# Gathered expert rows summed by four 64x64 products on TensorE's quarters in place of two products of the whole array

## The chip, the core and the metric

The program runs on one core of one Trainium2 chip. The metric is the time of one execution on the device, in microseconds (us). The engines are TensorE (PE in the profile, PEld for its weight loads), VectorE (DVE), ScalarE (ACT), GpSimd (POOL) and SyncE (SP), and 16 DMA engines move data between HBM and on-chip memory.

## What is computed

One layer of a decoder trunk on 1024 tokens of 1024 features: a mixer (latent attention, a recurrent branch, differential attention), cross-attention to a memory, and a retrieval FFN. The change touches only the last step of the FFN. Cut to this:

```python
def peer_ffn(h, w_q, keys, u, v):
    # ... experts (b, s, 8 heads, 16) and gates g from product keys; n_blk = 8 blocks of 128 tokens
    def block(args):
        xt, et, gt = args
        act = jax.nn.gelu(jnp.einsum('td,thkd->thk', xt, u[et]), approximate=False)
        return jnp.einsum('thk,thkd->td', gt * act, v[et])
```

For every token 128 rows of u (1024 floats each) are gathered and multiplied with the token's h, and 128 rows of v are gathered and added up with the weights gt * act. All is float32.

## The kernel before, in words

The tokens go in 8 blocks of 128, one token to a partition. Each block has a *front* (norms, projections, attention, recurrence, cross-attention, the choice of experts) and a *retrieval*. The retrieval of block b-1 runs through the front of block b: the class `Pace` places its 128 positions between the pieces of the front, on PE, ACT and DVE each, by tables of stops written out by hand (`TENSOR_STOPS`, `VECTOR_STOPS`, `SCALAR_STOPS`). The last retrieval runs alone after the last front.

At position p of the retrieval, for a block of 128 tokens:

- POOL gathers one u row per token (`gather_u`, L810) and one v row per token (`gather_v`, L824), each a 128x1024 tile, into rings of 9 slots. `gather_v` waits until the row that held the slot has been summed (`v_used`, counted by PE, or `v_added`, counted by DVE).
- DVE multiplies the u row with h and reduces it to a dot product (L2052).
- ACT turns 8 dot products into activations (L1516), DVE multiplies them with the gates to `coef` (L2084), and ACT builds for each row a diagonal matrix `diag` = identity scaled by that row's coefficient per token (L1528; four buffers).
- PE adds the v row to the running sum `ps_sum` (two PSUM banks of 128x512) as `diag` times the v row, at L1267 in `add_row`. Every eighth row goes instead to DVE (L2074), and in the last 24 positions of the last block every second one, so that 887 rows are summed on PE.
- After a block's last row DVE adds `ps_sum` to `x_cur` (`sum_out`, L2092), PE waits for this (`fin_sum`) before it starts the next block's sum, and ACT and DVE do the final norm from `x_cur`.

Lines of the front that the text names, all on PE: L999 and L1018 are projections, L1066, L1067 and L1071 the projections up from the latents (L1067 has 64 rows of the array), L1114 and L1118 attention scores (L1118 has 32 rows), L1100 turns of the probabilities, L1126 probabilities times values, L1181 the output projections; L1905 is a DVE add of a 128x512 PSUM bank. A float32 product appears in the trace as two weight loads and two matmul records, so a row of L1267 is four of each. `w_ring` holds the weights that SP streams from HBM.

Of the kernel before, what the change touches and what calls it, by code (L numbers as in the profile page):

```python
# [16 lines left out]
ALU = mybir.AluOpType  # L17
# [28 lines left out]
HALF = 512  # L46
# [49 lines left out]
def on_vector(b, j):  # L96

    return j % SHARE == SHARE - 1 or (b == NB - 1 and j >= TAIL and j % 2)


def adds_before(b, j):

    return sum(on_vector((b * EXPERTS + j - 1 - i) // EXPERTS, (j - 1 - i) % EXPERTS) for i in range(b * EXPERTS + j))


def sums_before(b, j):

    return b * EXPERTS + j - adds_before(b, j)
# [180 lines left out]
def program(nc, x, wstream, columns, w_uq, w_ukv, w_gates, keys_t, ffn_gain, final_gain, mem, positions, pos_cols,  # L289
            rel_bias, diff_lambda, peer_u, peer_v, out):  # L290
    with ExitStack() as ctx:
        def sb(name, shape, dt=F32):
            return ctx.enter_context(nc.sbuf_tensor(name, shape, dt))

        def pb(name, cols):
            return ctx.enter_context(nc.psum_tensor(name, [P, cols], F32))

        def sem(name):
            return ctx.enter_context(nc.semaphore(name))
# [3 lines left out]
        u_rows, v_rows = rows[:, 0:U_RING, :], rows[:, U_RING:U_RING + V_RING, :]  # L303
# [17 lines left out]
        x_cur = sb("x_cur", [P, D])  # L321
# [26 lines left out]
        diag = sb("diag", [P, 4, P])  # L348
# [42 lines left out]
        ps_sum = pb("ps_sum", D)  # L391
# [58 lines left out]
        fin_sum, fin_sq, fin_made, fin_stored = sem("fin_sum"), sem("fin_sq"), sem("fin_made"), sem("fin_stored")  # L450
# [21 lines left out]
        def ge(eng, semaphore, value):  # L472

            if isinstance(value, int) and value <= 0:
                return
            eng.wait_ge(semaphore, value)
# [72 lines left out]
        def row_of(bp, p, lag):  # L549

            j = p - lag
            if j >= 0:
                return (bp, j) if j < EXPERTS else (bp, None)
            return (bp, None) if isinstance(bp, int) and bp == 0 else (bp - 1, j + EXPERTS)

        def row_slot(b, j, ring):

            return (b * EXPERTS + j) % ring

        def row_landings(b, j, ring):  # L560

            return 16 * ((b * EXPERTS + j) // ring + 1)
# [359 lines left out]
        def _(pe):  # L922
# [333 lines left out]
            def add_row(bp, p):  # L1256
                bp, j = row_of(bp, p, SUM_LAG)
                if j is not None and not on_vector(bp, j):
                    n = sums_before(bp, j)
                    pe.wait_ge(diag_made, n + 1)  # L1260
                    slot = row_slot(bp, j, V_RING)
                    pe.wait_ge(v_landed[slot], row_landings(bp, j, V_RING))
                    if j == 0:

                        ge(pe, fin_sum, bp)
                    for c in range(2):
                        ins = pe.matmul(ps_sum[:, c * 512:(c + 1) * 512], diag[:, n % 4, :], v_rows[:, slot, c * 512:(c + 1) * 512],  # L1267
                                        start=(j == 0), stop=(n == sums_before(bp + 1, 0) - 1), skip_group_check=True)
                    ins.then_inc(v_used, 1)

# [16 lines left out]
            def first_mla():  # L1287
                pe.wait_ge(cleared, 6)
                mla(0, 0)

            pace = Pace(add_row, opening, TENSOR_STOPS)
            pace.run(front | {"project_0": lambda b: first_project(), "project_1": lambda b: second_project(),
                              "mla_up": lambda b: first_up(), "mla_0": lambda b: first_mla()}, 0)
# [281 lines left out]
        def _(dve):  # L1575
# [478 lines left out]
            def position(bp, p):  # L2054
                if p < EXPERTS:
                    multiply_row(bp, p)
                if ends_block(bp, p, SUM_AT):
                    sum_out(bp - 1)
                    hand_last_ids(bp)
# [28 lines left out]
            def sum_out(bp):  # L2088

                dve.wait_ge(v_used, sums_before(bp + 1, 0) + SUM_SLOTS)  # L2090
                dve.wait_ge(v_added, adds_before(bp + 1, 0) + ADD_SLOTS)
                dve.tensor_tensor(x_cur[:, :], x_cur[:, :], ps_sum[:, :], ALU.add).then_inc(fin_sum, 1)  # L2092

            def scale_out(bp):

# [39 lines left out]
            pace.start(NB - 1)  # L2135
            pace.to(END)
            sum_out(NB - 1)
            scale_out(NB - 1)

# [81 lines left out]
```

## Time and profile before

| | |
|---|---|
| runs (3) | 3477.66, 3482.75, 3485.28 us, median 3482.75 |
| profiled execution | span 3488.4 us (no other time is shown for it) |
| PE busy | 2948.9 us, 85% |
| DVE, POOL, ACT busy | 2349.6, 2015.7, 812.5 us |
| L1267, the sums on PE | 3548 matmul records, busy 1727.6 us |
| DMA | 1345 MB, mean 386 GB/s over the span |

Busy time is the time in which an engine had an instruction running. The ends of matmuls are modelled, so neighbouring starts are the better measure of a matmul's rate. A window gives, for a stretch of the span, the busy time of each engine with the number of instructions, the granted TensorE clock as a share of 2.4 GHz, and what DMA moved.

### The profile page before, as it was taken

The numbers are of one execution on the slowest core, as the hardware profiler recorded it, in microseconds if no ns is written. First come the engines' busy times: TensorE is split into PE (matmuls) and PEld (weight loads), VectorE is DVE, ScalarE is ACT, GpSimd is POOL, SyncE is SP. The second block draws the span as 40 slices with busy tenths as digits, with TensorE's granted clock in tenths as the row PEclk, the third lists the DMA queues.
The fourth block names the chain that finished last, engine by engine and source line by source line (L and its number), as shares of the span: only waits on it lengthen the run. The fifth ranks groups of instructions, "written<-read, shape, count | busy, mean of one in ns | idle before, by whom it ended". The sixth has DMA issues, their size and how long they took to land.

```text
span 3488.4 us, 34790 instructions
## 1 busy us (share of the span) xinstructions
PE 2948.9 (85%) x10984; PEld 1651.9 (47%) x10984; DVE 2349.6 (67%) x5893; ACT 812.5 (23%) x1915; POOL 2015.7 (58%) x2085
## 2 busy tenths in 40 slices
PE   7876898888988898889997899888998889976675
PEld 6465455544545355534554456444564445522222
DVE  6229846886588765886578765886648865596555
ACT  3111411132211421133211322114221232211111
POOL 1004755666566765666565655665556655477775
PEclk9898999999999999999999999998999999999998
DMA  7788999999999999999999999999999999999998
GB/s 279 277 274 313 408 409 409 408 409 409 409 407 406 394 409 409 408 407 382 409 409 408 392 356 409 409 409 348 359 409 409 409 355 342 385 404 410 409 409 347
DMA packets 386971, 1345.09 MB, mean 386 GB/s; under 512 B 41762, under 2 KB 44834, under 8 KB 386148
## 3 DMA queue, kind: packets, MB, share of 16 engines
q0 software_dynamic: 294912, 1073.87, 78.1%
q1 hardware_dynamic: 90724, 264.79, 20.0%
q10 hardware_dynamic: 1152, 4.19, 0.3%
q8 instruction: 90, 1.47, 0.2%
q14 instruction: 93, 0.76, 0.1%
HBM read 1332.99 MB, written 35.39 MB: 392 GB/s over the span
## 4 chain that ended last, share of the span: by engine, by line
PE 38%; DMA 30%; DVE 15%; POOL 9%; issue 6%; ACT 3%; SPq 1%; DVEq 0%; POOLq 0%; ACTq 0%
PE ps_sum L1267 18%; DMA rows<-in_peer_u,ids_u 13%; DMA rows<-in_peer_v,ids_v 10%; PE ps_p L999 5%; POOL rows L824 5%; POOL rows L810 4%; DVE rows L2052 4%; PE ps_s L1181 4%; DMA rows<-in_peer_v,ids_u 3%; DMA w_ring<-packed 3%; PE ps_s L1118 2%; PE ps_p L1126 2%; DVE feat_b L1935 1%; DVE feat_b L1931 1%; PE ps_s L1114 1%
## 5 line engine op out<-in xcount | busy, mean ns | idle before, releaser
L1267 PE MATMUL ps_sum<-rows,diag 128*128 128x512 f32 x3548 | 1727.6, 629 | 267.1 <-DMA rows<-in_peer_v,ids_v 141.4
L2052 DVE CUSTOM_DVE_ANT_0 rows<-h_cur,rows 128x1024 f32<-128x1024 f32 x1024 | 1226.8, 1220 | 496.3 <-DMA rows<-in_peer_u,ids_u 483.3
L810 POOL DMA_INDIRECT rows<-in_peer_u,ids_u x1024 | 1012.3, 989 | 702.0 <-issue 483.3
L1267 PEld LDWEIGHTS ps_sum<-rows,diag 128*128 128x128 f32 x3548 | 671.0, 200 | 1155.7 <-issue 1005.7
L824 POOL DMA_INDIRECT rows<-in_peer_v,ids_v x512 | 490.3, 958 | 433.8 <-PE ps_sum L1267 277.6
L824 POOL DMA_INDIRECT rows<-in_peer_v,ids_u x512 | 498.2, 973 | 284.7 <-PE ps_sum L1267 144.2
L1528 ACT ACTIVATE diag<-ident,acts 128x128 f32<-128x128 f32 x887 | 324.7, 394 | 1049.4 <-PE ps_sum L1267 750.1
L999 PE MATMUL ps_p<-hT,w_ring 128*128 128x128 f32 x2944 | 358.7, 282 | 28.8 <-DMA w_ring<-packed 15.3
L999 PEld LDWEIGHTS ps_p<-hT,w_ring 128*128 128x128 f32 x2944 | 353.0, 198 | 61.2 <-issue 39.7
L1834 DVE CUSTOM_DVE_ANT_0 e<-ps_s,bias_t 128x256 f32<-128x256 f32 (+6 forms) x96 | 74.2, 773 | 176.3 <-PE ps_s L1118 73.7
L2074 DVE SCALAR_TENSOR_TENSOR x_cur<-rows,acts,x_cur 128x1024 f32<-128x1024 f32 x137 | 175.6, 1282 | 7.4 <-DMA rows<-in_peer_v,ids_v 7.3
L1905 DVE TENSOR_TENSOR x_next<-x_next,ps_s 128x512 f32<-128x512 f32 x32 | 21.9, 685 | 200.0 <-PE ps_s L1181 200.0
L1516 ACT ACTIVATE acts<-dots 128x8 f32<-128x8 f32 x128 | 26.6, 208 | 486.9 <-DVE dots L2052 486.6
L1181 PE MATMUL ps_s<-w_ring,hT 128*128 128x512 f32 x256 | 118.3, 608 | 14.2 <-DMA w_ring<-packed 7.4
L1441 ACT ACTIVATE e<-e,small 128x256 f32<-128x256 f32 (+6 forms) x96 | 75.4, 785 | 219.7 <-DVE small L1836 219.4
L999 PE MATMUL ps_p<-pT,w_ring 128*128 128x128 f32 x1024 | 118.8, 276 | 0.9 <-DMA w_ring<-packed 0.9
L999 PEld LDWEIGHTS ps_p<-pT,w_ring 128*128 128x128 f32 x1024 | 116.9, 192 | 5.4 <-issue 3.3
L1181 PE MATMUL ps_s<-w_ring,feat_b 128*128 128x512 f32 x256 | 114.8, 592 | 1.1 <-DMA w_ring<-in_wstream 1.1
L1935 DVE FIND_INDEX8 feat_b<-feat_b,e 128x8 uint32<-128x128 f32 (+1 forms) x384 | 103.4, 279 | 0.0
L1118 PE MATMUL ps_s<-k_diff,feat_a 32*128 32x512 f32 (+2 forms) x192 | 83.7, 543 | 16.9 <-DVE small L1836 16.8
L1314 ACT ACTIVATE feat_a<-ps_p 128x512 f32<-128x512 f32 (+2 forms) x48 | 26.0, 542 | 304.6 <-PE ps_p L999 304.5
L2052 DVE DVE_READ_ACCUMULATOR2_ANT dots<- 128x1 f32 x1024 | 84.4, 82 | 0.0
(288 smaller groups left out, 2376.2 us busy)
## 6 DMA issues: line engine op xcount, KB each, us to landing
w_ring<-packed SPq DMA_DIRECT2D x343, 512.0 KB
w_ring<-in_wstream SPq DMA_DIRECT2D x65, 512.0 KB
packed<-in_wstream SPq DMA_DIRECT2D x49, 512.0 KB, 8.2
rows<-in_peer_u,ids_u POOLq DMA_INDIRECT x1024, 14.9
rows<-in_peer_v,ids_u POOLq DMA_INDIRECT x512, 12.6
rows<-in_peer_v,ids_v POOLq DMA_INDIRECT x512, 19.3
bias_rows<-rows SPq DMA_DIRECT2D x5, 1024.0 KB, 12.1
bias_t<-in_x SPq DMA_DIRECT2D x8, 512.0 KB, 7.9
```

The costliest lines, as they stand in the source:

```text
L810: pool.indirect_dma_start(u_rows[:, slot, :], None, peer_u, bass.IndirectOffsetOnAxis(ap=ids_u[:, j:j + 1], axis=0)).then_inc(u_landed[slo ...
L824: pool.indirect_dma_start(v_rows[:, slot, :], None, peer_v, bass.IndirectOffsetOnAxis(ap=ids[:, j:j + 1], axis=0)).then_inc(v_landed[slot] ...
L999: ins = pe.matmul(dst, w[:, k, :], lhs[:, kt, :], start=(kt == 0), stop=(kt == KT - 1))
L1118: ins = pe.matmul(ps_s[:, c0:c1], q_diff[r:r + DK, half // 4, :], k_diff[r:r + DK, half // 4, c0:c1], start=True, stop=True)
L1181: pe.matmul(ps_s[:, n * 512:(n + 1) * 512], lhs[:, kt, :], w, start=(kt == 0), stop=(kt == KT - 1)).then_inc(w_used, 1)
L1267: ins = pe.matmul(ps_sum[:, c * 512:(c + 1) * 512], diag[:, n % 4, :], v_rows[:, slot, c * 512:(c + 1) * 512], start=(j == 0), stop=(n == ...
L1441: act.activation(buf[:, 0:keys_n], buf[:, 0:keys_n], ACT.Exp, bias=small[:, 32 + n:33 + n], accum_out=small[:, 48 + n:49 + n]).then_inc(s_ ...
L1528: act.activation(diag[:, n % 4, :], ident[:, :], ACT.Copy, scale=coef[:, j:j + 1]).then_inc(diag_made, 1)
L1834: run(dve.tensor_tensor_reduce(buf[:, 0:keys_n], ps_s[:, 0:keys_n], bias[:, 0:keys_n], 1.0, -3.0e38, ALU.add, ALU.max, small[:, 16 + n:17 ...
L1935: dve.max_index(i[:, first:first + 8], v[:, first:first + 8], s).then_inc(top_step, 1)
L2052: dve.tensor_tensor_reduce(row, h_cur[:, :], row, 1.0, 0.0, ALU.mult, ALU.add, dots[:, p:p + 1]).then_inc(u_used, 1)
L2074: dve.scalar_tensor_tensor(x_cur[:, :], v_rows[:, slot, :], coef[:, j:j + 1], x_cur[:, :], ALU.mult, ALU.add)\
```

## The change

In `add_row` each v row is now four products. Product (c, r) takes the row half r of the partitions (64 tokens) and column half c of the features; its weights are the 64x64 block of `diag` on that half, and its result goes to partitions 64c to 64c+63 of bank r of `ps_sum`. So the partition half of `ps_sum` now tells the column half of the output, and the bank tells the token half. In `sum_out` the one add becomes four that put the quarters back to their places in `x_cur`.

```diff
-                    for c in range(2):
-                        ins = pe.matmul(ps_sum[:, c * 512:(c + 1) * 512], diag[:, n % 4, :], v_rows[:, slot, c * 512:(c + 1) * 512],
+                    for c, r in ((0, 0), (0, 1), (1, 0), (1, 1)):
+                        own = slice(64 * r, 64 * r + 64)
+                        ins = pe.matmul(ps_sum[64 * c:64 * c + 64, r * HALF:(r + 1) * HALF], diag[own, n % 4, own],
+                                        v_rows[own, slot, c * HALF:(c + 1) * HALF],
                                         start=(j == 0), stop=(n == sums_before(bp + 1, 0) - 1), skip_group_check=True)
                     ins.then_inc(v_used, 1)
@@ sum_out
-                dve.tensor_tensor(x_cur[:, :], x_cur[:, :], ps_sum[:, :], ALU.add).then_inc(fin_sum, 1)
+                for c, r in ((0, 0), (1, 1), (0, 1), (1, 0)):
+                    own = x_cur[64 * r:64 * r + 64, c * HALF:(c + 1) * HALF]
+                    ins = dve.tensor_tensor(own, ps_sum[64 * c:64 * c + 64, r * HALF:(r + 1) * HALF], own, ALU.add)
+                ins.then_inc(fin_sum, 1)
```

Nothing is moved: the rows of the retrieval stand between the same pieces of the front. What stands on PE in the attention stage of block 6 (`e` the probabilities, `pT` their turn, `feat_a` queries, `rows` with the v row and `diag` the diagonal; xN counts matmuls of the source) was before:

```order
L1100 MATMUL ps_p<-ident,e 128x128 x7
L1267 MATMUL ps_sum<-rows,diag 128x512 x2
L1126 MATMUL ps_p<-v_mla,pT 128x64 x7
L1118 MATMUL ps_s<-k_diff,feat_a 128x512
L1118 MATMUL ps_s<-k_diff,feat_a 128x384
L1267 MATMUL ps_sum<-rows,diag 128x512 x2
L1118 MATMUL ps_s<-k_diff,feat_a 128x512
```

and is now:

```order
L1100 MATMUL ps_p<-ident,e 128x128 x7
L1268 MATMUL ps_sum<-rows,diag 64x512 x4
L1126 MATMUL ps_p<-v_mla,pT 128x64 x7
L1118 MATMUL ps_s<-k_diff,feat_a 128x512
L1118 MATMUL ps_s<-k_diff,feat_a 128x384
L1268 MATMUL ps_sum<-rows,diag 64x512 x4
L1118 MATMUL ps_s<-k_diff,feat_a 128x512
```

The runs of sums stay where they were, 45 in each of the blocks' bodies but the first (43) and the last (37), and each now has other forms on both sides. A product of the source is two loads and two matmuls in the built program, directly behind one another, so that both passes of one quarter stand ahead of the first pass of the next.

## Rows read from the trace of the kernel before

**Rows 1.** The page: busy time (us), share of the span, instructions.

```profile
PE 2948.9 (85%) x10984; PEld 1651.9 (47%) x10984; DVE 2349.6 (67%) x5893; ACT 812.5 (23%) x1915; POOL 2015.7 (58%) x2085
```

**Rows 2.** Windows of 100 us, from the span's start; the first line names the columns.

```profile
core 0: us, PE busy (x) PEld busy (x) DVE busy (x) ACT busy (x) POOL busy (x), PEclk, DMA share, GB/s
...
1200.00:1300.00 100.00, 95.99 (x364) 53.26 (x363) 60.98 (x137) 26.74 (x62) 62.92 (x65) 1.00 1.01 396
...
1600.00:1700.00 100.00, 94.38 (x371) 53.61 (x372) 63.20 (x140) 27.80 (x63) 60.78 (x62) 1.00 1.01 391
...
2000.00:2100.00 100.00, 94.93 (x331) 50.20 (x331) 60.54 (x138) 31.35 (x67) 56.13 (x59) 0.97 0.94 354
2100.00:2200.00 100.00, 95.65 (x416) 59.33 (x415) 50.53 (x126) 22.57 (x51) 56.50 (x59) 1.00 1.03 409
...
2400.00:2500.00 100.00, 93.77 (x299) 48.36 (x298) 56.50 (x121) 33.49 (x64) 50.66 (x51) 0.91 0.87 312
2500.00:2600.00 100.00, 98.39 (x448) 62.28 (x447) 53.07 (x104) 21.14 (x52) 58.25 (x62) 1.00 1.03 409
...
2800.00:2900.00 100.00, 86.55 (x324) 46.11 (x323) 63.95 (x126) 40.92 (x74) 54.30 (x56) 0.98 0.92 341
2900.00:3000.00 100.00, 98.68 (x374) 57.13 (x374) 51.13 (x111) 20.10 (x48) 54.32 (x58) 0.97 0.95 370
3000.00:3100.00 100.00, 82.53 (x281) 43.53 (x279) 73.32 (x220) 15.11 (x38) 58.94 (x61) 0.97 0.98 383
```

**Rows 3.** Timeline, PE in the last retrieval: start us, us, what, [idle before].

```profile
3210.42 1.95 PE L1267 MATMUL ps_sum<-rows,diag 128*128 128x512 f32 x4 [0.61 <-DMA rows<-in_peer_v,ids_u]
...
3212.98 1.95 PE L1267 MATMUL ps_sum<-rows,diag 128*128 128x512 f32 x4 [0.61 <-DMA rows<-in_peer_v,ids_u]
```

**Rows 4.** Chain that ended last, window 2400 to 2500 us, shares by line.

```profile
by line: PE ps_sum L1267 43.8%; PE ps_s L1118 13.6%; PE ps_p L1126 12.2%; PE ps_p L1100 7.1%; DMA w_ring<-packed 6.0%; PE ps_s L1181 5.4%; ACT pT L1314 4.1%; PE ps_s L1114 3.1%; DVE e L1867 1.2%; ACT e L1441 1.1%; DVE e L1834 1.1%; issue 0.
```

**Rows 5.** Waits, whole span: who for whom, us in total, times, longest.

```profile
POOL rows L824 <- PE ps_sum L1267: 421.8, 244, 12.0
```

**Rows 6.** Timeline, PE in an attention stage; "128*128" is the part of the array.

```profile
2421.54 3.42 PE L1267 MATMUL ps_sum<-rows,diag 128*128 128x512 f32 x4
...
2428.09 1.98 PE L1267 MATMUL ps_sum<-rows,diag 128*128 128x512 f32 x4
2430.00 1.77 PE L1118 MATMUL ps_s<-k_diff,feat_a 32*128 32x512 f32 x4
...
2436.91 1.88 PE L1267 MATMUL ps_sum<-rows,diag 128*128 128x512 f32 x4
2438.63 1.67 PE L1126 MATMUL ps_p<-v_diff,pT 128*128 128x64 f32 x14
2440.23 1.77 PE L1118 MATMUL ps_s<-k_diff,feat_a 32*128 32x512 f32 x4
```

**Rows 7.** Timeline, PE, two lines that alternate between parts of the array.

```profile
2328.66 0.49 PE L1066 MATMUL ps_p<-feat_a,wuq 128*128 128x128 f32 x2
2329.08 0.48 PE L1067 MATMUL ps_p<-feat_a,wuq 64*128 64x128 f32 x2
```

**Rows 8.** Groups: out<-in xcount, busy us, mean ns, idle before with releasers.

```profile
L999 PE MATMUL ps_p<-hT,w_ring 128*128 128x128 f32 x2944 | 358.7, 282 | 28.8 <-DMA w_ring<-packed 15.3 <-DVE hT L1742 13.2
```

**Rows 9.** DVE adds from PSUM, by line: ns min/median/max, first and last start.

```profile
L2092 DVE TENSOR_TENSOR x_cur<-x_cur,ps_sum x8: 1214/1219/1221, 727.1 to 3479.6; 128x1024 f32<-128x1024 f32 x8
...
L1905 DVE TENSOR_TENSOR x_next<-x_next,ps_s x32: 677/686/689, 170.3 to 3005.2; 128x512 f32<-128x512 f32 x32
```

**Rows 10.** Windows of L1267 alone: window, us, PE and PEld busy, PEclk, DMA.

```profile
2000.00:2100.00 100.00, 51.95 (x108) 20.55 (x109) 0.97 0.94 354
2400.00:2500.00 100.00, 49.07 (x95) 18.53 (x93) 0.91 0.87 312
2800.00:2900.00 100.00, 42.75 (x88) 15.81 (x88) 0.98 0.92 341
```

**Rows 11.** A window near the end, columns as in rows 2.

```profile
3440.00:3450.00 10.00, 7.27 (x10) 2.26 (x9) 7.17 (x12) 1.60 (x5) 7.72 (x8) 0.57 1.03 409
```

## The prediction

> **What bounds the kernel now.** I read the windows first, since the one share that the page gives PE, 85% [rows 1], mixes stages. Where sums run, DMA is mostly the limit: at its full share it moves 409 GB/s, as in the windows from 2100 and 2500 us, and a window that shows less lost time [rows 2]. Each position of the retrieval brings one u row and one v row of 128 tokens, and in the last block, where nothing else runs on PE, the sums start 2.56 us apart, each after a wait of about 0.6 us for its row [rows 3]. There PE is busy 1.95 us of 2.56 and a faster sum brings nothing.
>
> The windows in which DMA falls short are all windows in which PE is nearly full [rows 2]: 354 GB/s at 94.93 us busy, 312 at 93.77, 341 at 86.55, 370 at 98.68, 383 at 82.53, and 396 and 391 at 95.99 and 94.38 in two earlier ones. Written as time lost, (409 - GB/s) / 409 x 100 us, these are 13.4, 23.7, 16.6, 9.5, 6.4, 3.2 and 4.4 us, together **77 us**. The dips fall in the attention and cross stages of the later blocks. The chain of waits there names the sums with 43.8% of the window, then the front's own products on PE (L1118, L1126, L1100), then little else [rows 4]. The link to DMA is the ring of v rows: the gather at L824 waited 421.8 us in all for a sum at L1267 to release its slot, ahead of every other wait on this ring [rows 5]. The opening runs below 409 GB/s too, but has no sums, and the change can't reach it. So a PE that costs nothing would bring at most 77 us, and the end of the kernel is reached through DMA.
>
> **What a sum costs.** One gathered row is two instructions in the source, four matmuls in the trace (each f32 product is done as two loads of weights and two passes of the moving rows). Four of them follow one another at 1.72 us when the next work has the same form (2436.91 to 2438.63 [rows 6]), so 0.43 us each. Where the granted clock falls to its lower level, 1.2 GHz, the same four take twice this, 3.42 us from first start to last end (at 2421.54 [rows 6]).
>
> **What is changed, part by part.** Per row PE gets eight loads and eight matmuls in place of four and four, each matmul still with 512 moving columns. A matmul's time follows its columns and not its height: four of the 32x512 form at L1118 are busy 1.77 us, four of the full 128x512 form 1.88 [rows 6]. One product of 64x64 therefore streams for 2 x 0.43 = 0.85 us, and all hangs on **how many of the four run at the same time**. They use four different quarters of the array, the two upper and the two lower row halves write to different banks, and nothing in the program orders them. The trace of before has no place where two products stand on disjoint parts of the array, so the price is bounded from both sides: all four together, 0.85 us a row; one after the other, 4 x 0.85 = 3.41 us.
>
> Full overlap also needs 8 loads and 8 matmuls to be issued in 0.85 us. The densest pairs in these rows are the 14 of L1126, which take 1.60 us from their start to the next line's, 0.114 us a pair (2438.63 to 2440.23 [rows 6]), and eight such pairs are 0.91 us; most of this is the load of 128 columns, where the new ones have 64. I take **0.90 us a row**, a saving of 1.71 - 0.90 = 0.81 us.
>
> The Trainium skill bears on this (TensorE: Matmul & The Clock Gate, Part 3, Packing small matmuls): it reports 16 tiles of 32x32 at 10.6 times the rate of one after the other, which would be the full overlap. No run here shows it, and nothing says that it was f32.
>
> **Switches of form.** The rows stand between the products of the front, which use the full array, in 45 runs a block, mostly of one to three rows (the order listing). Where neighbours differ in form today, it costs: L1066 and L1067 alternate between 128 and 64 rows, and start 0.42 us apart for two 128-column matmuls [rows 7]; in a stream of one form such a matmul takes 0.12 us (358.7 us over 2944 [rows 8]), so 0.24 for two, and a switch costs about **0.18 us**. A second place agrees for one direction: a row followed by L1118's 32-row form takes 1.91 us to the next start, in place of 1.72 (2428.09 to 2430.00 [rows 6]). A run of sums now has two switches, 0.4 us rounded up; between 0 (a load still pulled ahead) and 0.4, I take the upper end. 45 runs in a block of some 410 us are 11 in 100 us, so 4.4 us of PE in each window.
>
> **The last add on VectorE.** One add of 128x1024 at 1.22 us becomes four of 64x512. The nearest row is the add of 128x512 from PSUM at L1905, 0.686 us [rows 9]; with 64 partitions I expect no less, so 4 x 0.68 = 2.7 us, 1.5 us more for each of 8 blocks. At the end of the kernel nothing covers it: **+1.5 us**. In seven blocks PE waits for this add before its next block's first row, up to 7 x 1.5 = 10.5 us on PE, but the nine slots of v rows give cover (at 2.56 us a row [rows 3] a delay of 1.5 us doesn't empty them); I take +2 and keep 10.
>
> **The sum for full overlap.** The records of L1267 in the three worst windows are 108, 95 and 88, so 27, 24 and 22 rows [rows 10]. Freed on PE: 27 x 0.81 - 4.4 = 17.5; 24 x 0.81 - 4.4 = 15.0; 22 x 0.81 - 4.4 = 13.4 us. Against losses of 13.4, 23.7 and 16.6 this pays at most 13.4 + 15.0 + 13.4 = 41.8 us, and the four smaller windows their 23.5 (9.5 + 6.4 + 3.2 + 4.4), in all 65 us. Not all comes through: behind the sums stand the scores, the softmax on ScalarE and VectorE and the turns, in a fixed order with the rows, and a front that runs ahead within a window can't use time freed in the next one. I take two thirds, 43 us, and keep 20 and 77 as ends. With +1.5 and +2: **-40 us**. The span is 3488.4 us, the median of the runs 3482.75, 5.65 us below it; the runs' own time of the profiled execution isn't shown, so I take the difference from the median: 3482.75 - 40 = **3443 us**.
>
> What is late next is DMA itself in the first of the three windows (17.5 against 13.4), and still PE, with the front's products, in the other two. The granted clock may fall where PE now idles more: in the last block, where every second row went to VectorE and PE was 38% busy (1.95 us in 5.1), a window shows 0.57, a mix of both levels [rows 11]. A row at 1.2 GHz would then cost 1.8 us, still under 2.56, so it does harm only at the start of a crowded stage. That is inside the third not taken.
>
> **Rival 1, overlap only in pairs (slower).** If a matmul may not start before the one ahead of it in the program has started, the second pass of a product waits for the first on its own quarter, and everything behind it waits too. Then only the second pass of one product and the first of the next overlap: the products start 0.43 us apart, a row costs 4 x 0.43 = 1.71 us as today, and each run ends one pass (0.43 us) later, because the full array must wait for the last quarter. With the switches this is 0.43 + 0.36 = 0.8 us more per run and nothing gained. It decides wherever PE is full: nine windows of 100 us stand in rows 2, with 11 runs each, 9 x 11 x 0.8 = 79 us; with 1.5 for the add and less 5 for slack, +75 us: **3558 us**. The ends are +45 (half of the runs covered) and +150 (all 45 runs of the later blocks, and the lower clock's share). For it: the regular 0.43 us of the passes shows that PE takes them strictly one behind the other on one part of the array. Against it: nothing in the trace shows such a block between different parts.
>
> The same page of the Trainium skill (Part 3) says that matmuls start and end in program order and that only weight loads are pulled ahead. By that rule this rival would be the result; its measurements of many tiles had one matmul per tile, and so do not decide it.
>
> The Trainium skill (TensorEngine Tiling (Array Packing), Key Properties) says that changing the tiling mode drains the engine. By rows 7 this is 0.18 us a switch, so the trace agrees in kind.
>
> **Rival 2, no overlap at all.** PE busy 2948.9 + 887 rows x (3.41 - 1.71) = 4457 us, plus an estimate of 140 us for opening and end, out of the 540 us in which PE is idle today (3488.4 - 2948.9): **about 4600 us**. It would be so if the f32 passes, or two streams from the same 64 partitions, shut out the other quarters.
>
> **Rival 3, no difference.** Full overlap, but a lower clock and the switches eat what is freed, or DMA's dips have the softmax chain behind them: within 7 us of 3483. The chain of waits speaks against it, with 85% of the worst window on lines of PE (43.8 + 13.6 + 12.2 + 7.1 + 5.4 + 3.1) [rows 4].
>
> **How the numbers follow.** Full overlap 0.48 (3405 to 3465 by itself), pairs 0.32 (3528 to 3630), none 0.12, no difference 0.08. A difference under 0.2%, 7 us, can't be told from none here. Full overlap gives faster 0.45 and 0.03 within 0.2%; pairs give slower 0.30 and 0.02 within; none is slower. So faster 0.45, same 0.13, slower 0.42. The range leaves out the case without overlap and the far end of the pairs: 3400 to 3590.
>
> **What would show it.** Right: the weight loads of L1268 stand some 0.1 us apart instead of 0.43 (four products' worth in under 1 us), the busy time of the sums near half of 1727.6 us, DMA in the windows near 2000 to 3000 us above 380 GB/s, and the add at the end 2.7 us. Pairs: loads every 0.2 to 0.43 us with a row still 1.7 us, a later end of each run, DMA dips deeper and wider. No overlap: a row of 3.4 us and PE full from 400 us to the end. The forecast is wrong, too, if a switch costs much more than 0.18 us in the 64x64 form, which no row shows.

## The result

The changed kernel takes **3508.49 us** (median of 4 runs, 3502.89 to 3530.76), the kernel before 3484.02 us in the same comparison: ratio **1.0082**, 95% interval 1.0059 to 1.0105. It is slower by 0.8%, where 1.1% faster was forecast. The profiled execution has a span of 3501.1 us, against 3488.4.

The page of the profile after: busy time of the engines, then the span in 40 slices with PE's busy share and its granted clock in tenths. The last line is the costliest group on PE.

```profile
PE 2611.7 (75%) x14532; PEld 1309.8 (37%) x14532; DVE 2361.6 (67%) x5917; ACT 807.0 (23%) x1915; POOL 2006.3 (57%) x2085
...
PE   7876787778867787768877788678887789855654
...
PEclk9897798778978898877987798887897778967665
...
L1268 PE MATMUL ps_sum<-rows,diag 64*64 64x512 f32 x7096 | 1203.7, 785 | 487.7 <-DMA rows<-in_peer_v,ids_v 261.6
```

PE is 337 us less busy (2948.9 in [rows 1]), and the sums 524 us less (1727.6 before). So the sums did become faster, and all other products on PE, which nobody changed, became slower: they are busy 1408.0 us (2611.7 - 1203.7) in place of 1221.3 (2948.9 - 1727.6), 187 us more. What else changed is the mean granted clock: 0.947 of 2.4 GHz over the span before, 0.808 after. The windows that answer to [rows 2]:

```profile
1200.00:1300.00 100.00, 85.06 (x486) 42.95 (x478) 61.34 (x139) 26.30 (x62) 61.57 (x65) 0.91 1.02 404
...
2000.00:2100.00 100.00, 87.69 (x464) 42.39 (x467) 65.05 (x144) 30.68 (x65) 56.73 (x60) 0.89 0.95 360
...
2400.00:2500.00 100.00, 87.84 (x382) 42.16 (x382) 57.97 (x125) 35.18 (x66) 53.11 (x54) 0.71 0.83 296
...
2800.00:2900.00 100.00, 83.93 (x383) 36.40 (x380) 64.08 (x126) 40.34 (x78) 57.33 (x56) 0.76 0.91 332
2900.00:3000.00 100.00, 90.14 (x504) 48.08 (x503) 56.10 (x122) 27.86 (x62) 57.98 (x60) 0.88 0.94 360
3000.00:3100.00 100.00, 70.76 (x423) 31.88 (x421) 70.49 (x199) 15.29 (x39) 55.92 (x59) 0.85 1.02 405
```

At 1200, 2000 and 3000 us DMA moves more than before (404, 360 and 405 against 396, 354 and 383 GB/s), at 2400, 2800 and 2900 us less (296, 332 and 360 against 312, 341 and 370). The clock is lower in all of them, and it fell furthest at 2400 and 2800 us, from 0.91 and 0.98 to 0.71 and 0.76. The same window of time doesn't hold quite the same work in both traces, so the next comparison goes by work.

**One attention head at either clock.** The same piece of work is found in both traces: from the values of the last latent head (L1126 on `v_mla`) to those of the first differential head (`v_diff`), with the same four gathered rows between, in three runs. Two windows of the kernel before, block 5 and block 6, columns as in [rows 2]:

```profile
2004.12:2017.52 13.40, 12.71 (x44) 6.61 (x42) 7.14 (x16) 6.11 (x11) 9.59 (x10) 0.98 0.82 291
2424.79:2438.63 13.84, 13.15 (x47) 6.63 (x46) 7.49 (x16) 6.14 (x11) 9.02 (x9) 1.00 0.82 275
```

and the same two pieces after:

```profile
2013.58:2024.39 10.81, 9.46 (x62) 4.29 (x58) 6.41 (x14) 6.68 (x16) 8.00 (x9) 1.00 0.96 345
2427.15:2446.97 19.82, 19.13 (x66) 8.00 (x62) 7.55 (x16) 6.96 (x14) 9.90 (x10) 0.50 0.72 240
```

In block 5 PE keeps 2.4 GHz and the head takes 10.8 us in place of 13.4: 2.6 us gained with four rows, 0.65 a row. By the prediction's terms, 0.81 a row less 0.4 a run, it would be 4 x 0.81 - 3 x 0.4 = 2.0 us, so this head did a little better than forecast. In block 6 PE runs at 1.2 GHz all through and it takes 19.8 us in place of 13.8. One such head loses more than two others gain. Of these two pieces the timeline after shows the parts (start in us, duration, engine, line, operation, tiles): L1126, L1118 and the runs of rows L1268, first in block 5, then in block 6.

```profile
2016.54 1.09 PE L1268 MATMUL ps_sum<-rows,diag 64*64 64x512 f32 x8
2017.99 1.55 PE L1118 MATMUL ps_s<-k_diff,feat_a 32*128 32x512 f32 x4 [0.36 <-DVE small L1838]
2019.47 1.95 PE L1268 MATMUL ps_sum<-rows,diag 64*64 64x512 f32 x16
2021.35 0.66 PE L1100 MATMUL ps_p<-ident,e 128*128 128x128 f32 x4
...
2023.37 1.09 PE L1268 MATMUL ps_sum<-rows,diag 64*64 64x512 f32 x8
2024.39 0.32 PE L1126 MATMUL ps_p<-v_diff,pT 128*128 128x64 f32 x1
...
2427.15 3.25 PE L1126 MATMUL ps_p<-v_mla,pT 128*128 128x64 f32 x14
2430.32 3.35 PE L1118 MATMUL ps_s<-k_diff,feat_a 32*128 32x512 f32 x4
2433.61 1.99 PE L1268 MATMUL ps_sum<-rows,diag 64*64 64x512 f32 x8
```

**The same over all heads of the later blocks.** In blocks 4 to 7 the first L1126 of each of the eight heads cuts the attention stage into seven pieces like the two above, 28 in all. Together they take 305.2 us before, at a mean clock of 0.95, and 315.0 us after, at 0.76: 9.8 us more, of the 12.7 us by which the profiled span grew. The eight pieces that run at 0.97 or more after are 12.7 us shorter in sum than before; the five at 0.58 or less are 18.6 us longer; the other fifteen make up the rest, +3.9 us. PE is idle in 40.6 us of the 28 pieces, where it was idle in 31.7 before.

**The overlap is full.** A row, eight matmuls that stream 0.43 us each, takes 1.02 us to the start of the next line (2023.37 to 2024.39), and two rows 1.88 us (2019.47 to 2021.35), 0.94 a row. Narrower windows of the timeline show four of a row's matmuls starting together, and the other four together 0.48 us later:

```profile
2019.47 0.66 PE L1268 MATMUL ps_sum<-rows,diag 64*64 64x512 f32 x4
...
2019.95 0.61 PE L1268 MATMUL ps_sum<-rows,diag 64*64 64x512 f32 x4
```

At 1.2 GHz a row's eight are busy 1.99 us, and the front's products double, too: L1126 is 3.25 us in place of 1.67, L1118 3.35 in place of 1.77 [rows 6].

In the last retrieval, where nothing but sums runs on PE, the clock falls as well: from 3190 to 3440 us its mean is 0.68, where it was 0.96 before. The sums shown below run at 1.2 GHz, 1.98 us each, which is about what a row of the whole array took at 2.4 GHz [rows 3]. There it costs nothing: the sums start 2.56 us apart as before, and DMA moves 409 GB/s in that stretch in both kernels.

```profile
3211.40 1.99 PE L1268 MATMUL ps_sum<-rows,diag 64*64 64x512 f32 x8 [0.65 <-DMA rows<-in_peer_v,ids_u]
3213.96 1.98 PE L1268 MATMUL ps_sum<-rows,diag 64*64 64x512 f32 x8 [0.57 <-ACT diag L1530]
...
3490.71 2.80 DVE L2096 TENSOR_TENSOR x_cur<-ps_sum,x_cur 64x512 f32<-64x512 f32 x4
```

The last of these lines is the new add at the kernel's end, 2.80 us in place of 1.22 [rows 9].

### The profile page after: what moved, and what is told of

Its sections match the earlier page's. It is cut to its first block, busy times and chain, and to the rows that moved or that the text cites. A ratio compares the mean times of both kernels' runs of the same rounds, so it can differ in the third digit from the quotient of the medians.

```text
span 3501.1 us, 41910 instructions
## 1 busy us (share of the span) xinstructions
PE 2611.7 (75%) x14532; PEld 1309.8 (37%) x14532; DVE 2361.6 (67%) x5917; ACT 807.0 (23%) x1915; POOL 2006.3 (57%) x2085
## 4 chain that ended last, share of the span: by engine, by line
DMA 35%; PE 25%; DVE 23%; POOL 7%; issue 6%; ACT 2%; SPq 1%; DVEq 0%; POOLq 0%; ACTq 0%
DMA rows<-in_peer_u,ids_u 16%; DMA rows<-in_peer_v,ids_v 9%; PE ps_sum L1268 7%; DVE rows L2054 7%; DMA rows<-in_peer_v,ids_u 5%; POOL rows L824 4%; PE ps_s L1181 4%; POOL rows L810 3%; DMA w_ring<-packed 3%; PE ps_p L999 3%; PE ps_p L1126 2%; PE ps_s L1118 2%; DVE feat_b L1937 2%; DVE feat_b L1933 1%; PE ps_p L1100 1%
## 5 line engine op out<-in xcount | busy, mean ns | idle before, releaser
L1268 PE MATMUL ps_sum<-rows,diag 64*64 64x512 f32 x7096 | 1203.7, 785 | 487.7 <-DMA rows<-in_peer_v,ids_v 261.6
L810 POOL DMA_INDIRECT rows<-in_peer_u,ids_u x1024 | 1001.7, 978 | 722.2 <-issue 486.7
L1268 PEld LDWEIGHTS ps_sum<-rows,diag 64*64 64x64 f32 x7096 | 262.6, 162 | 1218.1 <-issue 896.8
L999 PE MATMUL ps_p<-hT,w_ring 128*128 128x128 f32 x2944 | 377.7, 289 | 30.4 <-DMA w_ring<-packed 23.9
L1181 PE MATMUL ps_s<-w_ring,hT 128*128 128x512 f32 x256 | 121.5, 615 | 18.6 <-DMA w_ring<-packed 9.1
L1118 PE MATMUL ps_s<-k_diff,feat_a 32*128 32x512 f32 (+2 forms) x192 | 100.8, 639 | 24.4 <-DVE small L1838 24.4
L1100 PE MATMUL ps_p<-ident,e 128*128 128x128 f32 x256 | 59.5, 345 | 57.6 <-ACT pT L1316 31.4
```

Of the source, the lines that this page charges most:

```text
L810: pool.indirect_dma_start(u_rows[:, slot, :], None, peer_u, bass.IndirectOffsetOnAxis(ap=ids_u[:, j:j + 1], axis=0)).then_inc(u_landed[slo ...
L999: ins = pe.matmul(dst, w[:, k, :], lhs[:, kt, :], start=(kt == 0), stop=(kt == KT - 1))
L1100: ins = pe.transpose(bank[:, (t - t0) * P:(t - t0 + 1) * P], src[:, t * P:(t + 1) * P], ident[:, :])
L1118: ins = pe.matmul(ps_s[:, c0:c1], q_diff[r:r + DK, half // 4, :], k_diff[r:r + DK, half // 4, c0:c1], start=True, stop=True)
L1181: pe.matmul(ps_s[:, n * 512:(n + 1) * 512], lhs[:, kt, :], w, start=(kt == 0), stop=(kt == KT - 1)).then_inc(w_used, 1)
L1268: ins = pe.matmul(ps_sum[64 * c:64 * c + 64, r * HALF:(r + 1) * HALF], diag[own, n % 4, own], v_rows[own, slot, c * HALF:(c + 1) * HALF], ...
```

## The experiments

The **clock theory**: PE time that the faster sums free in the crowded stretches turns into waits for the softmax; with less to do PE is granted 1.2 GHz for part of the stretch, and the front's products take twice as long; the gain is handed back. Its rivals: the **switch theory**, in which the 64x64 form costs the time by its switches and the longer add, and the **chain theory**, in which PE was never what held back these stretches. Every kernel below was timed in five rounds against the kernel before, in four comparisons in which that one stood at 3481.0 to 3483.4 us; the changed kernel itself has only the four runs above, against 3484.02. So kernels of different comparisons are best compared by their ratios. "Clock" is the mean granted clock of the profiled execution.

### Half of the sums, without tiles

```diff
-  ins = pe.matmul(ps_sum[:, c * 512:(c + 1) * 512], diag[:, n % 4, :], v_rows[:, slot, c * 512:(c + 1) * 512],
+  ins = pe.matmul(ps_sum[:, c * 512:c * 512 + 256], diag[:, n % 4, :], v_rows[:, slot, c * 512:c * 512 + 256],
```

> The kernel before with half of the feature columns left out of each row's sum on PE (two full-array products of 256 columns in place of 512): a row streams for 0.85 us, as the four overlapped 64x64 products do, but with no switch of form and with the old add on VectorE. Clock theory (what the faster sums freed was taken by the granted clock, which falls when PE has less to do): mean clock 0.80 to 0.85, the crowded windows again with clock dips, 3490 to 3515 us. Switch theory (the 64x64 form itself costs the time, by its switches and the longer add): the clock stays near 0.9 in the crowded stages and the time is 3435 to 3455 us.

Measured: 3483.59 us, ratio 1.0003 (0.9986 to 1.0021), clock **0.798**. With no tile, no switch and no new add, half of the streaming was taken away and the time didn't move; the clock fell as in the changed kernel. It came out 6 us below the clock theory's range and far above the switch theory's. The time alone would fit the chain theory. The pieces of the attention stage say more: the nine of the 28 that ran at full clock were 18.9 us shorter in sum than before, so PE does hold them back, and the three at 0.58 or less were 10.1 us longer; all 28 take 303.4 us (305.2 before) at a mean clock of 0.79. The windows of this kernel:

```profile
2000.00:2100.00 100.00, 88.78 (x327) 59.41 (x327) 61.28 (x140) 30.24 (x65) 54.34 (x58) 0.80 0.96 369
2400.00:2500.00 100.00, 83.68 (x315) 55.94 (x314) 61.65 (x131) 35.81 (x69) 55.44 (x58) 0.85 0.90 331
2800.00:2900.00 100.00, 83.30 (x302) 55.38 (x301) 60.96 (x122) 38.99 (x70) 53.48 (x55) 0.78 0.89 322
```

### An eighth of the sums

The same edit with 64 columns in place of 256.

> The kernel before with seven eighths of the feature columns left out of each row's sum on PE (64 columns in place of 512): a row streams for 0.21 us in place of 1.71, 1.5 us a row or some 1330 us of PE freed. If PE time in the crowded stages were the only cause of the 77 us of DMA loss: 3405 to 3420 us. Clock theory, in which freed time turns into waits and the waits into a lower clock for the front's own products: mean clock under 0.75 and 3450 to 3490 us.

Measured: **3535.78 us**, ratio 1.0159 (1.0146 to 1.0172), clock **0.680**. Taking away still more work makes the kernel slower, by 55 us against the kernel before. That is beyond the clock theory's 3450 to 3490 us and the opposite of what a PE bound at an unchanged clock would give. The chain theory has no place for it either. The 28 pieces take 355.1 us, 50 more than before, at a mean clock of 0.51: nearly all of the loss lies there. The head of block 6 again, in this kernel, and the window of its block 6 (columns as in [rows 2]):

```profile
2441.13:2457.44 16.31, 15.16 (x46) 10.20 (x45) 6.55 (x14) 6.97 (x16) 7.51 (x8) 0.50 0.72 227
...
2360.00:2790.00 430.00, 306.85 (x1409) 242.47 (x1408) 288.51 (x719) 104.81 (x236) 249.41 (x256) 0.67 0.98 377
```

The head runs at 0.50 throughout and takes 16.3 us, against 13.8 with full sums at 2.4 GHz. By its timeline the four rows take 3.7 us (7.2 before), for at this clock two rows of 64 columns still take 1.76 us (2452.45 to 2454.21) and not the 2 x 0.21 that I expected. Waits take 1.2 us (0.7 before), and the front's own products 11.5 us (6.0 before). So neither the sums' own time nor the softmax is the limit there; the front's products at 1.2 GHz are.

### The same PE time in tiles

Four products of 128x64 (both row halves of the array in each, half of the weights zero), same layout of `ps_sum` and same adds as the changed kernel:

```diff
-  for c, r in ((0, 0), (0, 1), (1, 0), (1, 1)):
-      ins = pe.matmul(ps_sum[64 * c:64 * c + 64, r * HALF:(r + 1) * HALF], diag[own, n % 4, own], v_rows[own, slot, ...],
+  for r, c in ((0, 0), (0, 1), (1, 0), (1, 1)):
+      ins = pe.matmul(ps_sum[64 * c:64 * c + 64, r * HALF:(r + 1) * HALF], diag[:, n % 4, 64 * r:64 * r + 64], v_rows[:, slot, ...],
```

> The changed kernel with four products of 128x64 tiles (all 128 rows of the array, half of them with zero weights), same layout of ps_sum and same adds: two products at a time, 1.71 us a row as before, the same 45 runs and switches a block, and PE as busy as before. Clock theory: clock back to 0.93 or more, time 3484 plus only switches and add, 3485 to 3505 us, the switches paid at full PE. Switch theory: the cost of the form stays and nothing is freed, 3515 to 3560 us. If column halves don't overlap, a row takes 3.4 us and the time is above 4400 us.

Measured: 3500.75 us, ratio 1.0055 (1.0036 to 1.0075), clock 0.946. And the changed kernel with four more products of zero weights behind each row (taken from the zero quarters of `ident`), meant to bring a row back to 1.71 us (in its trace it takes 1.77 inside a run and 1.83 to 1.87 with the end of the run):

```diff
+  for c, r in ((0, 0), (0, 1), (1, 0), (1, 1)):
+      own, other = slice(64 * r, 64 * r + 64), slice(64 - 64 * r, 128 - 64 * r)
+      ins = pe.matmul(ps_sum[64 * c:64 * c + 64, r * HALF:(r + 1) * HALF], ident[own, other], v_rows[own, slot, ...], start=False, ...)
```

> The changed kernel with each row's four products followed by four more of the same size whose weights are zero: PE spends 1.71 us a row again, all in 64x64 tiles, and the result is unchanged. Clock theory, with a clock that follows how long PE is busy: mean clock 0.93 to 0.95, time 3490 to 3510 us. If the clock follows how much of the array works or whether it works on zeros, it stays near 0.8 and the time is 3560 us or more. Switch theory: 3515 to 3560 us at a clock of 0.94.

Measured: 3497.03 us, ratio 1.0044 (1.0028 to 1.0061), clock 0.943. Both restore the mean clock, which here followed the time that PE works and not the share of the array, nor whether a product's weights are all zero. (The real weights are diagonals, so all but one in 64 or 128 of them are zero too: how dense weights would do isn't shown.) Eight useless matmuls a row make the changed kernel some 11 us *faster* (3497.0 against 3508.5, in two comparisons; the intervals of the ratios, 1.0028 to 1.0061 and 1.0059 to 1.0105, just touch). What is left over the kernel before, some 14 to 17 us, I put down to the form. The trace of the 128x64 kernel shows it:

```profile
2448.15 1.94 PE L1267 MATMUL ps_sum<-rows,diag 128*64 128x512 f32 x8
2450.01 1.77 PE L1126 MATMUL ps_p<-v_diff,pT 128*128 128x64 f32 x14
2451.72 1.77 PE L1118 MATMUL ps_s<-k_diff,feat_a 32*128 32x512 f32 x4
2453.41 3.65 PE L1267 MATMUL ps_sum<-rows,diag 128*64 128x512 f32 x16
2457.00 1.77 PE L1118 MATMUL ps_s<-k_diff,feat_a 32*128 32x512 f32 x4
```

A row before L1126 takes 1.86 us where it took 1.72, and L1126 behind it 1.71 where it took 1.60 [rows 6]: 0.14 + 0.11, so 0.25 us a run. Between two L1118, whose 32-row form was a switch before as well, a run costs no more than it did: two rows take 3.59 us (2453.41 to 2457.00), where 1.72 + 1.91 stood in [rows 6].

### The add alone

The kernel before with `sum_out` cut into four adds of 64x512 in the old places; unlike those of the changed kernel, each reads and writes the same partitions.

> The kernel before with only the last add of each block cut into four of 64x512 (same places): 2.7 us in place of 1.22, eight times. Prediction's term: +1.5 us at the end and +2 in the blocks, 3487 to 3488 us. If this add holds back PE's next block and the ring with it: +1.5 us in each block, 3494 to 3498 us. Clock theory: no change of clock, 0.947.

Measured: 3486.18 us, ratio 1.0011 (1.0000 to 1.0022), clock 0.934. The term is +2.8 us, somewhat less than the 3.5 taken, and hardly told from noise. The clock of 0.934 isn't told from the kernel before either, whose runs in this comparison show 0.936 to 0.946. The 32 adds have a median of 684 ns:

```profile
L2094 DVE TENSOR_TENSOR x_cur<-ps_sum,x_cur x32: 676/684/695, 721.0 to 3478.5; 64x512 f32<-64x512 f32 x32
```

### Less work in the crowded stretch alone

Rows 16 to 51 of a block run beside attention. First the kernel before with half the columns left out only there:

```diff
+  wide_row = 256 if 16 <= j < 52 else 512
```

> The kernel before with half of the feature columns left out only for rows 16 to 51 of each block (the stretch that runs beside attention), all other rows whole. It frees 32 x 0.86 = 28 us of PE a block in the crowded stages and takes away little of PE's work elsewhere. Clock theory: the clock in the stretch falls less than with half rows everywhere (0.80), the DMA dips shrink, and the time is 3445 to 3470 us, below the 3483.6 of half rows everywhere although more work is done. If PE isn't what holds DMA back there (the softmax chain is, as the rival without a difference says): 3478 to 3485 us.

Measured: **3477.70 us**, ratio 0.9979 (0.9965 to 0.9994), clock 0.901. A gain of 6 us, where I had expected 13 to 38. It is more than with half rows everywhere (0), though less work is left out, but the time lies at the lower end of the chain theory's range (3478 to 3485) and not in the clock theory's. What the trace adds is that the clock falls within the stretch itself: the 28 pieces run at 0.77, as with half rows everywhere (0.79), and take 304.4 us. Then three variants of the changed kernel in which the zero products stay (a row of some 1.8 us) except in rows 16 to 51, in these rows only from block 3 on (and in the last retrieval), and in rows 16 to 79:

```diff
-  for c, r in ((0, 0), (0, 1), (1, 0), (1, 1)):
+  for c, r in ((0, 0), (0, 1), (1, 0), (1, 1)) if not 16 <= j < 52 else ():
```

> The changed kernel with the second four products of zero weights kept, except for rows 16 to 51 of each block: 64x64 products once in the crowded stretch, twice elsewhere; the result is unchanged. Clock theory: below the 3497 us of the products twice everywhere by what the half rows in the same stretch bring, 3465 to 3490 us. Chain theory: 3493 to 3500 us, as with the products twice everywhere.

> As the kernel with single products in rows 16 to 51, but only beside the fronts of blocks 3 to 7, where PE is crowded, and in the last retrieval: early blocks, where DMA is the limit, keep the clock up with double products. Clock theory: equal to it or up to 5 us faster. Chain theory: 3493 to 3500 us.

> As the kernel with single products in rows 16 to 51, but in rows 16 to 79, so that the cross-attention stage, where PE was busy 98%, has single products too. Clock theory: the clock is lower in more of the block, so no faster than with rows 16 to 51, within 5 us of it; if PE time in the cross stage counts, up to 10 us faster. Chain theory: 3493 to 3500 us.

Measured: 3500.05 us (ratio 1.0050, 1.0034 to 1.0065), 3505.49 (1.0069, 1.0050 to 1.0088) and 3502.13 (1.0049, 1.0031 to 1.0068), clocks 0.906, 0.910 and 0.881. My expectation failed for the first two, and the third, within 5 us of the first, held. A busy PE outside the stretch doesn't carry the clock through it: the 28 pieces of the first run at 0.76, as in the changed kernel, and take 318.9 us. By times alone the first fits the chain theory too (3493 to 3500 us), and the other two lie 5 and 2 us above it. What they rule out is a cure from outside the stretch.

### How many zero columns

The changed kernel with zero products of fewer columns behind each row, everywhere:

```diff
+  part = 256        # 128, 384
+      ins = pe.matmul(ps_sum[64 * c:64 * c + 64, r * HALF:r * HALF + part], ident[own, other], v_rows[own, slot, c * HALF:c * HALF + part], ...)
```

> The changed kernel with each row's products followed by four of 256 columns with zero weights, half as much as in the kernel with the products twice: a row takes 1.28 us at the full clock, between 0.9 (after) and 1.71. The result is unchanged. Clock theory, in which freed time is handed back through the clock: mean clock between 0.808 and 0.943, about 0.89, and the time stays in 3495 to 3510 us, since less work and a lower clock cancel. If there is a best point at which the clock still holds: 3480 to 3490 us.

> The changed kernel with pads of 384 columns of zero weights behind each row: 1.5 us a row at the full clock. The points so far: no pads 3508 us at clock 0.80, 256 columns 3481 at 0.919, 512 columns 3497 at 0.943. A clock theory with a best point between: 3483 to 3492 us at clock 0.93 to 0.94, since the clock gains little above 256 columns and PE's work grows. If the 3481 of 256 columns was chance: 3495 to 3505 us.

> The changed kernel with pads of 128 columns: 1.1 us a row. Clock theory with a best point near 256: clock 0.85 to 0.89, time 3485 to 3500 us. If what the pads bring isn't the clock but some order between the sums and the front's products that any pad gives: 3475 to 3483 us at this pad too.

and with 256 only in rows 16 to 51 and 512 elsewhere:

> The changed kernel with pads of 512 columns of zero weights behind each row, of 256 in rows 16 to 51: a row of 1.28 us in the crowded stretch, 1.71 elsewhere. Clock theory: between the kernels with none (3500) and full (3497) pads in that stretch, 3493 to 3502 us, clock 0.92. If there is a best point at which the clock still holds: 3480 to 3490 us.

The last two columns are the 28 pieces of the attention stage in the profiled execution, their time and mean clock (305.2 us at 0.95 in the kernel before).

| zero columns a row | us | ratio (interval) | clock | pieces, us | their clock |
|---|---|---|---|---|---|
| 0 (the changed kernel) | 3508.49 | 1.0082 (1.0059 to 1.0105) | 0.808 | 315.0 | 0.76 |
| 128 | 3492.73 | 1.0026 (1.0002 to 1.0051) | 0.858 | 323.2 | 0.79 |
| **256** | **3481.11** | 0.9990 (0.9978 to 1.0003) | 0.919 | 299.0 | 0.91 |
| 384 | 3492.50 | 1.0024 (1.0009 to 1.0040) | 0.927 | 316.1 | 0.90 |
| 512 | 3497.03 | 1.0044 (1.0028 to 1.0061) | 0.943 | 310.4 | 0.97 |
| 0 in rows 16 to 51, 512 else | 3500.05 | 1.0050 (1.0034 to 1.0065) | 0.906 | 318.9 | 0.76 |
| 256 in rows 16 to 51, 512 else | 3479.39 | 0.9995 (0.9983 to 1.0007) | 0.933 | 295.0 | 0.93 |

There is a best point on both sides of which the time rises. As I read it, with fewer zero columns the clock falls, and with more PE's own work fills up. With 256, everywhere and in the stretch alone, the clock theory as I had put it, a gain cancelled by the clock, failed (3495 to 3510 and 3493 to 3502 us), and a best point, the other case that I had named, is what came out; 384 and 256 in the stretch missed its ranges by less than 1 us. At 128 the time was as expected and not the 3475 to 3483 us that an effect of order alone would give, though its interval and that of 256 just touch. At 256 the kernel is 27 us faster than the changed one (two comparisons, whose intervals are well apart), for 887 x 8 matmuls that add nothing. The last two rows and 512 everywhere differ only within the stretch and show the same shape (3500, 3479, 3497), so it is PE's work in the stretch itself that counts. In the kernel with 256 columns the piece of block 5 used above takes 11.8 us at full clock:

```profile
1999.95:2011.75 11.80, 11.11 (x94) 5.51 (x90) 7.05 (x16) 6.55 (x14) 8.68 (x10) 1.00 0.93 329
```

10.8 with no zero columns, 13.4 before: part of the gain is kept, and the clock holds there. Block 6 of the same kernel still had heads at 0.72 to 0.88. Neither this kernel nor the one with 256 in the stretch beats the kernel before beyond the intervals.

## Why the prediction was wrong, step by step

- **The bound.** DMA outside the crowded stretches, PE in them: half right. The DMA losses do lie where PE is crowded. The ring's wait for the sums, which I took for the link, didn't shrink with them (421.8 us before, 423.3 after). Of the seven windows that I called nearly full, two had PE busy only 86.55 and 82.53 us [rows 2]: waits were in them already. And "a PE that costs nothing would bring at most 77 us" took PE's clock for given: with an eighth of the sums' columns the kernel lost 55 us.
- **The overlap.** Right, if a little dearer: 0.94 us a row in a run of two and 1.02 alone, both with the end of the run, where 0.90 was taken. The bound of issue didn't bind: eight loads of 64 columns take 0.21 us in the group below (of the changed kernel). Rival 1, overlap in pairs, gave the right direction and a time 50 us too high for a reason that isn't so.

```profile
2456.95 0.21 PEld L1268 LDWEIGHTS ps_sum<-rows,diag 64*64 64x64 f32 x8 [0.17 <-issue]
```

The Trainium skill's rule that matmuls start in program order (TensorE: Matmul & The Clock Gate, Part 3) would, as I had read it, have held the later quarters behind the second pass of the first. The measured 0.94 us a row says that it doesn't for these f32 passes. The timeline goes further: four matmuls start at 2019.47 and four at 2019.95, though the program has both passes of a quarter ahead of the next quarter's first. If a quarter takes one pass at a time, as the price of a row says, then the first pass of the last quarter started before the second pass of the first, and the starts are not in program order. Which record is which pass the trace doesn't tell.

- **The switches.** Two a run at 0.18 us were taken, rounded to 0.4 a run; 0.25 is measured in the 128x64 form beside L1126, and nothing more than before between two L1118. In time they cost more than I saw: I charged them only to the windows, against what was freed there, and the kernels with PE time unchanged show 3500.75 - 3486.18 = 14.6 us for them (tiles of 128x64 against the add alone, same comparison); whatever else that form costs is in this number too.
- **The last add.** Right in size: 2.80 us for four, +2.8 us in the time against +3.5.
- **The step that failed** is "it does harm only at the start of a crowded stage. That is inside the third not taken". I had named the mechanism (rival 3, a lower clock eats what is freed, chance 0.08), though only as no difference, within 7 us of 3483, and looked for it where DMA is the limit and it is harmless. In the crowded stretch I took PE to be busy by nature. It was busy because the sums filled its waits for the softmax. With shorter sums more of the waits come out (31.7 us idle in the 28 pieces before, 40.6 after, 46.4 with half the columns), the clock falls (0.95 to 0.76 and 0.79), and the front's products take up to twice their time. The 43 us that this step kept came out as zero (half the columns, ratio 1.0003) or negative (the tiles).
- **The sum as measured**: add +2.8, switches +14.6, and the rest to 24.5 us (3508.49 - 3484.02), some 7 us, on the freed time itself. The rest is a difference between comparisons with intervals of some 0.2% (7 us) each, so it shows only that the freed time was no gain.

The Trainium skill (TensorE: Matmul & The Clock Gate, Part 1) describes the lower clock as the default that activity lifts, and warns of waits between bursts of matmuls. The traces agree with the first: 0.947 before, 0.808, 0.798 and 0.680 where PE's work was cut, 0.943 where it was filled with zeros. I had read the page for the rate of tiles and not for this.

What stays open: why the clock falls in one head and not in the next, with the same kinds of work and waits in both (block 5 and block 6 above); why the tiles with 0.9 us a row lose some 7 us more than their switches and add, where half columns at 0.85 us lose nothing; and what sets the best point, since at 128 and 384 zero columns the pieces took longer than with none (323.2 and 316.1 us against 315.0, one profiled execution each) at a higher clock.

## What to carry to other kernels

Before making matmuls faster, ask what the granted clock will be when they are: where PE is busy in a stretch only because the work that you mean to shorten fills its waits (87 to 94% in two windows here), a shorter form can turn into a lower clock for everything beside it, and the kernel may get slower. Test it cheaply: leave out half of the columns and look at the time and the clock before any new form is written. Where the clock is the cost, matmuls on zeros in the same place can pay, but only up to a point, and here they only brought back what the change had lost.

## What the runs showed of the hardware

- Four f32 products of 64x64 by 512 columns on the four quarters of the array run together: 0.94 us a row in runs of two at 2.4 GHz, 1.02 for a row alone with its end, against 1.72 for two products on the whole array. Their matmuls start four at a time. Products of 128x64 run together in pairs as well: four of them, with the switch behind them, take 1.86 us, the time of two whole products and not of four.
- A run of another tile form between full-array products cost 0.25 us for both ends beside L1126, and nothing more where its neighbours were of a third form already.
- The mean granted clock followed how long PE works: whole array or tiles, all-zero or diagonal weights made no difference (0.946 and 0.943 with PE time about as before, 0.947 before).
- With 7/8 of the columns of its sums on PE left out, the kernel took 1.6% more time, at a mean clock of 0.680.
